# Input and first weight unit loaded and multiplied in alternating quarters, with 14 constant products at the very beginning

## What is computed

```python
def rms_norm(x, g):
    xf = x.astype(jnp.float32)
    y = xf * lax.rsqrt(jnp.mean(xf * xf, -1, keepdims=True) + EPS)
    return (y * g.astype(jnp.float32)).astype(x.dtype)

zp = rms_norm(hp, norm_mix[layer])          # layer 0: hp is x_prompt, hs is x_sample
...
proj = h @ w_in                             # 1024 x 2048; pooling input, q, k, v
...
bias = jnp.transpose(table[rel_bucket(jnp.maximum(dist, 0))], (2, 0, 1))[None]
```

## Time and profile before

| | us |
|---|---|
| median of 3 runs | 1551.88 (1550.71 to 1552.65) |
| the profiled execution | 1552.58 |
| its span in the profile | 1550.8 |
| TensorE busy | 1434.8 (93%) |
| first product of TensorE | 13.33 |
| first product of unit 1 (tile 2) | 29.27 |

### The profile page before, as it was taken

The page is one execution under the profiler, slowest core; times in us unless marked ns, Lnnn a source line. Parts: engine busy times, 40 slices in busy tenths (PEclk is TensorE's granted clock), DMA queues, the critical chain, the costliest instruction groups (busy, mean ns, idle before and its releaser), DMA issues. The chain is left out here.

```text
span 1550.8 us, 28326 instructions
## 1 busy us (share of the span) xinstructions
PE 1434.8 (93%) x11834; PEld 1201.3 (77%) x11834; DVE 697.3 (45%) x949; ACT 504.0 (33%) x708; POOL 392.6 (25%) x470
## 2 busy tenths in 40 slices
PE   6998789999999999798998989889789999999996
PEld 5765468888888888687777777777678888888885
DVE  5345443333333232857667576575534323233222
ACT  5233343332323122424424334243233322323220
POOL 2002312222221000624335343243311222212001
PEclk9999689999999999899999999999899999999998
DMA  7374403423233312002011110111033232233311
GB/s 263 143 258 163 131 28 109 150 93 106 83 118 113 112 66 80 27 29 82 28 55 37 68 61 28 55 50 47 1 123 109 82 108 83 106 118 112 108 42 55
DMA packets 30171, 140.89 MB, mean 91 GB/s; under 512 B 4329, under 2 KB 4585, under 8 KB 17802
## 3 DMA queue, kind: packets, MB, share of 16 engines
q1 hardware_dynamic: 30090, 139.75, 26.0%
HBM read 128.63 MB, written 11.11 MB: 90 GB/s over the span
## 5 line engine op out<-in xcount | busy, mean ns | idle before, releaser
L1445 PE MATMUL P<-zh,wh 128*128 128x260 f16 x1728 | 333.1, 274 | 18.6 <-DVE wl L981 13.3
L1445 PE MATMUL P<-zl,wh 128*128 128x260 f16 x1728 | 333.0, 274 | 0.0
L1445 PE MATMUL P<-zh,wl 128*128 128x260 f16 x1728 | 332.9, 274 | 0.0
L1445 PE MATMUL P<-arena,wh 128*128 128x260 f16 x1920 | 295.4, 276 | 6.0 <-DVE arena L1161 4.7
L981 DVE SCALAR_TENSOR_TENSOR wl<-stage,wh 128x2048 f16<-128x2048 f32 (+1 forms) x77 | 190.0, 2468 | 220.3 <-ACT wh L640 195.9
L1445 PEld LDWEIGHTS P<-arena,wh 128*128 128x128 f16 x1920 | 187.0, 98 | 39.3 <-DVE arena L1161 5.7
L1445 PEld LDWEIGHTS P<-zh,wh 128*128 128x128 f16 x1728 | 166.3, 97 | 50.0 <-issue 23.7
L1445 PEld LDWEIGHTS P<-zh,wl 128*128 128x128 f16 x1728 | 167.4, 97 | 26.5
L1445 PEld LDWEIGHTS P<-zl,wh 128*128 128x128 f16 x1728 | 167.3, 97 | 26.3
L1445 PE MATMUL P<-arena,wl 128*128 128x260 f16 x960 | 186.1, 275 | 0.0
L1784 PE MATMUL P<-arena 128*128 128x128 f32 x1152 | 156.1, 288 | 26.9 <-issue 16.9
(11 more groups left out here) (264 smaller groups left out, 1651.2 us busy)
## 6 DMA issues: line engine op xcount, KB each, us to landing
stage<-w_gu SPq DMA_DIRECT2D x44, 1024.0 KB, 4.8
stage<-w_in SPq DMA_DIRECT2D x24, 1024.0 KB, 5.7
stage<-w_dn SPq DMA_DIRECT2D x16, 1408.0 KB, 6.0
arena<-cache_k SPq DMA_DIRECT2D x32, 256.0 KB, 3.3
stage<-w_out SPq DMA_DIRECT2D x8, 1024.0 KB, 7.2
arena<-cache_v SPq DMA_DIRECT2D x32, 256.0 KB, 3.3
arena<-delta_state SPq DMA_DIRECT2D x8, 512.0 KB, 3.5
o_ds<-arena SPq DMA_DIRECT2D x8, 512.0 KB, 6.8
```

The lines of the kernel that those rows point to most:

```text
L1445: mm = nc.tensor.matmul(pm[j][:, c, :], w[:, wslot, o:o + 128], x[:, k, c * CH:(c + 1) * CH], start=(k == 0 and w is wh and x is xh), stop ...
```

## The change

The input comes in four quarters of two tiles, and weight unit 0 in four quarters of its k steps; SP issues them alternately, each with a semaphore of its own, and unit 1 right behind them, ahead of the small loads. ScalarE and VectorE split quarter by quarter, and the squares of all eight tiles come behind the last quarter. TensorE takes each step k for both tiles of the unit before the next k, and the statistics after both tiles. Ahead of everything TensorE multiplies `onesD` by itself 14 times into a PSUM bank that nobody reads; GpSimd signals `warm` when `onesD` is filled.

```diff
@@ -39,6 +39,7 @@
 
 UQ = KD * 256 // 4
 UNIT = KF * 128
+WARM = 14
 
 PHASES = (("in0", 8, 2, KD * 256), ("out0", 4, 2, KD * 256), ("gu0", 22, 2, KD * 256), ("dn0", 8, 1, UNIT),
           ("in1", 16, 2, KD * 256), ("out1", 4, 2, KD * 256), ("gu1", 22, 2, KD * 256), ("dn1", 8, 1, UNIT))
@@ -217,7 +218,10 @@
         scratch = nc.dram_tensor("bias_scratch", (4, 128 * SKEW), f32).ap()
 
 
-        x_in, x2_in, c_in = sem("x_in"), sem("x2_in"), sem("c_in")
+        x_in, c_in = sem("x_in"), sem("c_in")
+        warm = sem("warm")
+        xq_in = [sem(f"xq_in{i}") for i in range(4)]
+        w0_in, w0_hi, w0_lo = [sem(f"w0_in{i}") for i in range(3)], sem("w0_hi"), sem("w0_lo")
         kv_in = [sem(f"kv_in{i}") for i in range(NKV)]
         w_in = [sem(f"w_in{i}") for i in range(2)]
         consts = sem("consts")
@@ -317,9 +321,11 @@
                 weights(w_out0, FIRST_UNIT["out0"] + u, u % 2, u, WORDS[FIRST_UNIT["out0"] + u])
 
             sp.dma_start(par[:, :], params).then_inc(x_in, 16)
-            sp.dma_start(hT[:, 0:4, :], xT[:, 0:4, :]).then_inc(x_in, 16)
-            project_in(0)
-            sp.dma_start(hT[:, 4:8, :], xT[:, 4:8, :]).then_inc(x2_in, 16)
+            for q in range(4):
+                sp.dma_start(hT[:, 2 * q:2 * q + 2, :], xT[:, 2 * q:2 * q + 2, :]).then_inc(xq_in[q], 16)
+                sp.dma_start(stage[:, 0, q * UQ:(q + 1) * UQ], w_in0[ORDER0[0]][:, q * UQ:(q + 1) * UQ]
+                             ).then_inc(w0_in[q] if q < 3 else w_in[0], 16)
+            project_in(1)
             sp.dma_start(pt[:, :], pages).then_inc(c_in, 16)
             sp.dma_start(oh[0:33, :], onehot).then_inc(c_in, 16)
             sp.dma_start(tab[0:33, :], rel_tab).then_inc(c_in, 16)
@@ -331,7 +337,6 @@
             for h in range(H0):
                 sp.dma_start(sel[32 * h:32 * h + 16, :],
                              sel64.rearrange("(b h m) c -> h b m c", h=H0, m=2)[h]).then_inc(c_in, 16)
-            project_in(1)
             sp.wait_ge(c_in, 16 * 11)
             project_in(2)
             for n in range(NKV):
@@ -424,7 +429,7 @@
             link(nc.gpsimd.affine_select(out=ident[:, :], in_=ident[:, :], compare_op=ALU.not_equal, fill=1.0, base=0,
                                          pattern=[[-1, 128]], channel_multiplier=1))
             nc.gpsimd.memset(ones[:, :], 1.0)
-            nc.gpsimd.memset(onesD[:, :], 1.0 / D)
+            nc.gpsimd.memset(onesD[:, :], 1.0 / D).then_inc(warm, 1)
             nc.gpsimd.memset(onesH[:, :], 1.0 / 128)
             nc.gpsimd.memset(epsc[:, 0:1], EPS * WS * WS)
             nc.gpsimd.memset(epsc[:, 1:2], EPS)
@@ -674,15 +679,16 @@
                 nc.scalar.activation(wh[:, u % 2, 0:WORDS[u]], stage[:, u % 2, 0:WORDS[u]], ACT.Copy, scale=WS
                                      ).then_inc(hi_ready, 1)
 
-            for half in range(2):
-                act.wait_ge(*((x_in, 32) if half == 0 else (x2_in, 16)))
-                for k in range(4 * half, 4 * half + 4):
+            act.wait_ge(x_in, 16)
+            for q in range(4):
+                act.wait_ge(xq_in[q], 16)
+                for k in range(2 * q, 2 * q + 2):
                     nc.scalar.activation(zh[:, k, :], hT[:, k, :], ACT.Copy, scale=par[:, NORM[0] + k:NORM[0] + k + 1]
                                          ).then_inc(z_hi, 1)
-                if half == 0:
-                    split_hi(0, 0, WORDS[0])
-                    square_x(0)
-            for k in range(1, KD):
+                act.wait_ge(w0_in[q] if q < 3 else w_in[0], 16)
+                nc.scalar.activation(wh[:, 0, q * UQ:(q + 1) * UQ], stage[:, 0, q * UQ:(q + 1) * UQ], ACT.Copy, scale=WS
+                                     ).then_inc(w0_hi if q < 3 else hi_ready, 1)
+            for k in range(KD):
                 square_x(k)
             split_hi(1, 1, WORDS[1])
             act.wait_ge(consts, 1)
@@ -994,11 +1000,13 @@
                                                scalar=par[:, NORM[b] + k:NORM[b] + k + 1], in1=zh[:, k, :],
                                                op0=MUL, op1=SUB).then_inc(z_lo, 1)
 
-            for k in range(4):
-                norm_lo(0, k)
-            split_lo(0, 0, WORDS[0])
-            for k in range(4, 8):
-                norm_lo(0, k)
+            for q in range(4):
+                for k in range(2 * q, 2 * q + 2):
+                    norm_lo(0, k)
+                dve.wait_ge(*((w0_hi, q + 1) if q < 3 else (hi_ready, 1)))
+                nc.vector.scalar_tensor_tensor(out=wl[:, 0, q * UQ:(q + 1) * UQ], in0=stage[:, 0, q * UQ:(q + 1) * UQ],
+                                               scalar=WS, in1=wh[:, 0, q * UQ:(q + 1) * UQ], op0=MUL, op1=SUB
+                                               ).then_inc(w0_lo if q < 3 else lo_ready, 1)
             dve.wait_ge(sq_ready, 2)
             link(nc.vector.tensor_tensor(ssq[:, :], sq8[:, 0, :], sq8[:, 1, :], ADD))
             for k in range(2, KD):
@@ -1034,7 +1042,7 @@
             dve.wait_ge(act_step, 1)
             link(nc.vector.scalar_tensor_tensor(out=nlam, in0=lame[:, 1:2], scalar=-LAM0, in1=lame[:, 0:1],
                                                 op0=ADD, op1=SUB))
-            dve.wait_ge(x_in, 32)
+            dve.wait_ge(x_in, 16)
             link(nc.vector.tensor_scalar(subw, par[:, P_SUB:P_SUB + 1], 1 - LAM0, None, MUL))
             dve.nop().then_inc(lam_ready, 1)
             leave_in(3)
@@ -1540,13 +1548,19 @@
                     nc.tensor.matmul(P[:, 4 + m, 0:w], qkv[part, h, qt * 128:(qt + 1) * 128], qkv[part, 4 + h, 0:w],
                                      start=True, stop=True).then_inc(s_ready, 1)
 
-            pe.wait_ge(hi_ready, 1)
-            pe.wait_ge(lo_ready, 1)
-            product(0, 0, 0, zh, zl, KD, 256, ready=z_ready(0)).then_inc(mm_done, 1)
-            product(1, 0, 128, zh, zl, KD, 256, range(6))
+            pe.wait_ge(warm, 1)
+            for i in range(WARM):
+                nc.tensor.matmul(P[:, 7, 0:128], onesD[:, :], onesD[:, :], start=True, stop=True)
+            for k in range(KD):
+                pe.wait_ge(z_lo, k + 1)
+                if k % 2 == 0:
+                    pe.wait_ge(*((w0_lo, k // 2 + 1) if k < 6 else (lo_ready, 1)))
+                for n in range(2):
+                    mm = product(n, 0, 128 * n, zh, zl, KD, 256, (k,))
+                    if k == KD - 1:
+                        mm.then_inc(mm_done, 1)
             pe.wait_ge(consts, 1)
             statistics(0)
-            product(1, 0, 128, zh, zl, KD, 256, range(6, KD)).then_inc(mm_done, 1)
             strip(0)
             strip(1)
             unit("in0", 0, 1, zh, zl, between=last_strips)
```

## The result

The changed kernel is slower: 1554.38 us median against 1550.76 us, 22 runs of each side by side, ratio 1.0022 with a 95% interval of 1.0012 to 1.0031. By the ratio that is 3.4 us longer (1.9 to 4.8), where 1.3 us less was predicted. The profiled execution took 1553.3 us (span 1551.5).

The account below looks back on a forecast made before the run. TensorE, busy 93% of the span, was taken as the bound. Strips 3.3 us earlier less 2.0 us lost to the clock gave 1.3 us off the 1551.9 median: 1550.6 us, range 1547.4 to 1552.6.

Parts of the forecast that it names:

- First product, 7.8 at the high pace: Kernel start: TensorE's first product at 7.8 us instead of 13.3, at 0.109 us each from the start or nearly.
- First tiles ahead of the statistics: TensorE ends the first two tiles at 18.3 us instead of 26.9, before the sums of squares at 19.6.
- Statistics late by 1.3 us: After the first tiles: squares follow the last input quarter, so TensorE waits 1.3 us and statistics start at 19.6.
- A copy held through the split of unit 1: Strip tables: one GpSimd copy is blocked until VectorE's split of unit 1 ends at 22.1 us.
- the 0.30 taken: Strip tables: the five copies left after the split take 0.30 us each, giving tables at 23.6 us.
- A second wait, released by GpSimd, of 2.5 to 3 us: Before strip(0): TensorE stands still from 20.7 to 23.6 us, until GpSimd's table copies are done.
- The constants bring nothing here and 1.95 where uncovered: Kernel start: 14 constant products save 1.95 us that falls into later waiting; worth 1.95 without that cover.
- the upper bound of 1.0 us for quarters: Input and unit 0 loads: 2 KB rows cost at most 1.0 us more for unit 0's 1024 KB; taken as 0.
- The row that I judged by: Profile row of page-sized cache loads: 243 GB/s at queue share 0.80, 304 at full share, against 432.
- the clock's price: Strips and part of tile 2: two close waits bring TensorE to the slow pace, costing 2.0 us.
- the low clock stays: Rival: strip(0) to strip(3) keep the clock low after the wait before the strips; 1555 us, chance 0.07.
- the tables come later: Rival: slower 2 KB rows and copies at 0.76 us put tables at 25.9, clock falls too; 1552.9 us, chance 0.12.

Follow-up runs that it names:

- e2: Changed kernel with no constant products (WARM 14 to 0); ratio 1.0006 to the kernel before.
- e7: Kernel before with 36 constant products of 128 rows at its start, nothing else changed; ratio 0.9990 to the kernel before.
- e13: e10 with the input in two transfers, unit 0 in one, 24 constant products, splits still quartered; ratio 0.9986 to the kernel before.
- e11: e7 with the 36 constant products made from 33 rows instead of 128; ratio 1.0027 to the kernel before.
- e9: Changed kernel with strip(0) and strip(1) moved behind tile 2, ScalarE's split of unit 2 ahead of them; ratio 1.0027 to the kernel before.
- e12: Kernel before with 21 idle GpSimd memsets ahead of the eight table copies, so TensorE waits for the tables; ratio 1.0041 to the kernel before.
- e4: Changed kernel with the bias table loaded right behind the parameters on its own semaphore, GpSimd waiting for that alone; ratio 1.0002 to the kernel before.
- e10: e4 with 6 more constant products ahead of the statistics; ratio 1.0006 to the kernel before.
- e5: Changed kernel run again unaltered, with a second trace; ratio 1.0031 to the kernel before.
- e1: Changed kernel with unit 1's load put back behind the eleven small loads; ratio 1.0026 to the kernel before.
- e6: e4 with unit 1's load put back behind the small loads; ratio 1.0006 to the kernel before.
- e15: e10 with unit 1's load put back behind the small loads; ratio 0.9992 to the kernel before.
- e3: Changed kernel with 6 more constant products ahead of the statistics and 10 ahead of strip(0); ratio 1.0007 to the kernel before.
- e14: e13 with unit 1's load put back behind the small loads; ratio 0.9991 to the kernel before.

## Why the prediction was wrong

**Right.** *First product, 7.8 at the high pace*: 8.25, at 0.11 us each. But all 14 constants ran at the low pace (0.44 us each) and end at 8.08 rather than 7, so the pace rose just in time. *First tiles ahead of the statistics*: yes. *Statistics late by 1.3 us*: 1.71. *A copy held through the split of unit 1*: 2.15 us, and the rest at 0.29 and 0.20, near the 0.30 taken. *A second wait, released by GpSimd, of 2.5 to 3 us*: 2.43. *The constants bring nothing here and 1.95 where uncovered*: at tile 2, e2 (nothing) and e7 (1.8).

**Wrong by 1.9 us of lead: the small transfers.** I took the upper bound of 1.0 us for quarters as 0, and the bound was too low as well. By my sum the third quarter lands at 9.0; ScalarE waited for it until 11.76. The fourth was used right behind it at 13.74, not 11.6, and everything that hangs on it moved by about 2 us: squares' end 19.8 for 17.8, sums 21.8 for 19.6, first tiles 20.2 for 18.3, the small loads 19.8 for 17.7, strip(0) 25.5 for 23.6. The lead was 1.4 and not 3.3 us. The row that I judged by was of cache loads in a running queue, 304 GB/s at full share; the quarters moved 197 at a share of 0.82, so 240. The Trainium skill's page "DMA: Bandwidth & Descriptors", section "Bandwidth", advises transfers of 1 MiB or more; the trace agrees in kind, with 325 GB/s for the quarters against 427 for e13's larger ones in the same stretch. No run shows the fourth quarter in use at 11.6: with large transfers it is 13.85 (e13). What is shown is the rate; that large transfers would have kept the lead is not.

**Wrong by 2.6 us: the clock's price.** The mechanism was named (two waits, then strips), and the size was taken from the 3.9 us that the first tiles needed to speed up. It is 4.6 us: 1.4 of lead became 3.2 of loss between strip(0) and tile 2's end, 2.2 of it in the strips (4.63 for 2.42) and 2.4 in tile 2. The 2.0 was too small by the prediction's own terms: strips that take twice as long cost 2.35 alone. The failed argument is that 3.9 us of work after the wait bring the pace up: the strips ran at 1.2 GHz for 4.6 us without raising it, and tile 2 then ran 5.0 us before the pace rose. In e11 products of 33 rows left the pace low, and in e9 it fell in a row of them. The low stretch lasted 10 us and not 4. The rival *the low clock stays* had this mechanism right, with a chance of 0.07; it asked for 6.6 us of slow work to lose and for 13 to be over 3.1 us slower, since it still held 3.3 us of lead. With 1.4 us, 10 were enough. The rival *the tables come later* had the strips right (25.9, measured 25.48) and kept the price of 2.0.

So 1.3 us faster became 3.2 us slower at tile 2: 1.9 from the lead and 2.6 from the price. e12 has the price by itself, e4 the same kernel without the second wait.

**Still open.** The end of a kernel doesn't always follow its lead at tile 2. Twelve of the fifteen rows do, within 1.7 us; e2 ends 3.3 us better, and e4 and e10 2 to 4 us worse. For e10 the traces show where it went; for e2 and e4 they show only that it was behind 120 us, and e4's profiled execution, the fastest of its twelve, still ended early (1546.65). Later waits with falls of the clock come out differently: behind the same wait of 3.21 us the first products take 0.59 us in the kernel after and in e4, at the low pace, and 0.39 in the kernel before and 0.38 in e10. The twelve executions of e4 spread up to 1557.79. Open too is when a wait brings the clock down. From 20 to 60 us every wait of 2.17 us or more stood ahead of a fall (after, e5, e1, e2, e6, e9, e10, e12), but one of 2.46 us behind the constants of e15 did not, nor did 1.88 us in e7. And in e3 and e15 it fell in the strips with 0.27 and 0.66 us of waiting ahead of them, where in e4, e10, e13 and e14 the same strips ran without a fall. Each of these is one trace.

## What to carry to other kernels

Before moving work forward, ask what the engine does after it: a lead that ends in a wait is lost, and if the wait brings TensorE's clock down, it turns into a loss. Price a fall of the clock by all the work until the trace shows it risen, strips of few rows in full. Price small first transfers by the rate that a trace shows for such, not by that of large ones. Send the tiny load that a long chain hangs on first of all (it moved tile 2 by 6.9 us here), and look for the next thing that waits: the gain was not found again at the end. Constant products in a kernel's idle start brought something at tile 2 only where the first tiles were the late ones.

## What the hardware showed

- Thirty-six fp32 products of 33 rows ran at the low pace to the last, 0.44 us each over 15.7 us (e11); 36 of 128 rows were at the high pace from about 5 us on (e7). When the rise comes varies: the 14 of 128 rows took 6.14 us in the kernel after, 5.64 in e5 and 4.98 in e1.
- Sixteen strip products together were followed by the fall to 0.50 with TensorE busy throughout (e9, one trace).
- A wait of 1.88 us between two runs of 128-row products changed nothing (e7), nor did one of 2.46 us behind the constants of e15 or one of 1.32 us before the statistics (e4). Behind waits of 2.2 to 2.6 us the level went to 0.50 for 7 to 10 us (e1, e6, e12), 0.3, 0.6 and 1.2 us after the wait had ended. Beyond the wait the fall cost 3.3 us in e12 and 4.6 us in the kernel after.
- The same bytes in alternating quarters moved at 197 and 325 GB/s in the first two stretches, in halves at 419 and 423.
- A GpSimd copy of 33x32 took 2.15 us beside VectorE's split of 2.38 us, 0.59 under its sums and 0.20 with VectorE idle (kernel after, e4).
